# Attention probabilities split by query and turned by DMA, with slots of their own in a hand-written order

## The reference

```python
u = rmsnorm(h); proj = u @ w_in        # columns of attention A, attention C and the mixer B
oa = banded_attention(qa, ka, va, 128, 1, ...)          # 4 heads of 64, with sinks
for window, dil in ((128, 1), (512, 4), (2048, 16)):    # attention C, 4 heads, keys by stride
    o, s = dilated_banded_attention(qc, kc, vc, window, dil, tab_c)
# banded attention, per block of 128 queries, keys of this block and of the previous one:
logits = einsum('nbqhgd,nbshd->nbhgqs', qb, kb) + bias
probs = exp(logits - max); out = einsum('nbhgqs,nbshd->nbqhgd', probs, vb) / sum(probs)
xbc, z -> causal_dwconv, silu, ssd_chunked (chunks of 128 tokens), gated rmsnorm      # mixer B
h = h + concat(oa, ob, oc) @ w_out
h = h + square(relu(rmsnorm(h) @ w_up)) @ w_down
```

## Time and profile before

| | |
|---|---|
| median of 3 runs | 2439.88 us (2436.4 to 2441.14) |
| profiled run | 2438.68 us, span 2436.8 us |
| TensorE busy | 2354.4 us, 97% |
| VectorE / ScalarE / GpSimd busy | 1194.3 / 838.8 / 296.0 us |
| DMA | 419.64 MB, queue q1 56.9% of 16 engines |
| column stage | about 308 to 677 us |
| MLP stage | from about 740 us on |

### The profile page before, as it was taken

How to read it: one execution, slowest core, us unless ns; L and a number is a source line. 1 busy time by engine, 2 the same in 40 slices (tenths; PEclk the granted TensorE clock), 3 DMA queues, 4 the chain that set the end, 5 groups by cost and what they waited for, 6 DMA issues and landing times. The chain is left out here.

```text
span 2436.8 us, 42346 instructions
## 1 busy us (share of the span) xinstructions
PE 2354.4 (97%) x17150; PEld 1363.1 (56%) x17150; DVE 1194.3 (49%) x2673; ACT 838.8 (34%) x1579; POOL 296.0 (12%) x317
## 2 busy tenths in 40 slices
PE   9899889999899999999999999999999999999999
PEld 5456445554345555444555554445555456888887
DVE  5567465655647666742655563145555522322222
ACT  5544244555445454331433321033334111210210
POOL 0111223112011212001121100101111001000000
PEclk9999999999999999999999999999999999999999
DMA  7646496785477867884565564445554553222222
GB/s 254 238 168 226 169 231 174 211 233 178 144 228 201 218 208 230 257 266 159 141 159 160 166 200 153 158 132 128 159 173 156 177 162 117 88 96 96 96 96 85
DMA packets 396561, 419.64 MB, mean 172 GB/s; under 512 B 130319, under 2 KB 325391, under 8 KB 396112
## 3 DMA queue, kind: packets, MB, share of 16 engines
q1 hardware_dynamic: 396368, 416.94, 56.9%
HBM read 280.01 MB, written 118.96 MB: 164 GB/s over the span
## 5 line engine op out<-in xcount | busy, mean ns | idle before, releaser
L2423 PE MATMUL core_dense<-core_u,tok_ring 128*128 128x512 f16 (+2 forms) x4800 | 863.9, 340 | 7.8 <-DVE core_u L2008 7.5
L2423 PEld LDWEIGHTS core_dense<-core_u,tok_ring 128*128 128x128 f16 x4800 | 465.8, 98 | 377.9 <-DVE core_u L2008 11.4
L2423 PE MATMUL core_dense<-core_r_hi,tok_ring 128*128 128x512 f16 (+2 forms) x2560 | 650.1, 339 | 1.7 <-DVE core_r_lo L2027 1.7
L2423 PE MATMUL core_dense<-core_r_lo,tok_ring 128*128 128x512 f16 (+2 forms) x1280 | 434.1, 339 | 0.0
L2423 PEld LDWEIGHTS core_dense<-core_r_hi,tok_ring 128*128 128x128 f16 x2560 | 250.4, 98 | 196.8 <-DVE core_r_lo L2027 2.7
L2423 PE MATMUL core_dense<-tok_u,tok_ring 128*128 128x512 f16 x1104 | 257.7, 390 | 14.8 <-PEq L811 10.9
L1806 ACT ACTIVATE core_r<-core_dense 128x512 f32<-128x512 f32 (+2 forms) x160 | 82.2, 514 | 472.2 <-PE core_dense L2423 472.1
L2024 DVE TENSOR_TENSOR core_r<-core_r 128x512 f32<-128x512 f32 (+2 forms) x160 | 96.7, 604 | 291.1 <-ACT core_r L1806 290.7
L732 PE MATMUL tok_prod<-tok_w_hi,tok_u 128*128 128x512 f16 (+1 forms) x768 | 196.3, 345 | 4.1 <-DVE tok_u L601 4.1
L2423 PEld LDWEIGHTS core_dense<-tok_u,tok_ring 128*128 128x128 f16 x1104 | 107.3, 100 | 146.0 <-issue 24.8
L2423 PEld LDWEIGHTS core_dense<-core_r_lo,tok_ring 128*128 128x128 f16 x1280 | 125.2, 98 | 93.9 <-issue 0.7
(11 more groups left out here) (318 smaller groups left out, 2593.8 us busy)
## 6 DMA issues: line engine op xcount, KB each, us to landing
tok_ring<-scratch_kept_w SPq DMA_DIRECT2D x262, 512.0 KB, 4.5
scratch_kept_w<-tok_ring SPq DMA_DIRECT2D x72, 512.0 KB, 5.6
core_staged<-in_w_up SPq DMA_DIRECT2D x32, 512.0 KB, 4.7
core_staged<-in_w_down SPq DMA_DIRECT2D x32, 512.0 KB, 4.3
out_tok<-tok_tok SPq DMA_DIRECT2D x16, 644.0 KB, 3.0
core_piece<-in_c_kt SPq DMA_DIRECT2D x32, 288.0 KB, 3.9
core_piece<-in_c_v SPq DMA_DIRECT2D x16, 576.0 KB, 4.4
scratch_sums<-core_o SPq DMA_DIRECT2D x64, 132.0 KB, 3.7
```

The costliest lines, as they stand in the source:

```text
L2423: ins = pe.matmul(bank, w[:, k, part, :], s, start=first and j == 0, stop=last and j == 2, skip_group_check=True)
```

## The change

Attention's unit is cut into three with slots of their own: `S` (scores, bias, maxima, exponential), `T` (halves and turn) and `O` (product with the values, store). In `T` ScalarE and VectorE split `p` as it stands, by query, into `p_half` in SBUF, and two transposing DMAs on SyncE's queue write its turned form `p_t`, again in SBUF. TensorE's transposes, banks 3 and 4 for them and `p_hi`, `p_lo` are gone; the product uses bank 4. The plan is new:

- first 16 tiles: one every four quarters, `T` two and `O` six quarters after `S`; the 12 of the first block: one every five; MLP stage: one every two units, `T` one and `O` three units after `S`.
- the scans no longer stand behind all attention but among it, a chunk every 14 quarters or 10 units; the sums for the joins have a slot of their own (`sums`).
- the bias has two slots and is loaded once per run of tiles of one kind (`bias_runs`); the sampled keys always use banks 3 and 0.

```diff
+        def place_attention(beside, group, at, step, halved, valued):
+            was = None
+            for n in reals[group]:
+                beside[at].append(("S", n, 0, 0))
+                if was is not None:
+                    beside[at - step + valued].append(("O", was, 0, 0))
+                beside[at + halved].append(("T", n, 0, 0))
+                was, at = n, at + step
+            beside[at - step + valued].append(("O", was, 0, 0))
+            return at
...
-            for slot in att_slots(0, att_end[0]):
-                beside[at].append(slot)
-                at += 3
-            for n, slot in enumerate(att_slots(att_end[0], att_end[1])):
-                beside[at].append(slot)
-                at += 4 - n % 2
+            at = place_attention(beside, 0, 4 * COL_AHEAD + 1, 4, 2, 6)
+            last = place_attention(beside, 1, at + 3, 5, 2, 6)
...
-                beside[at].insert(0, first)
-                beside[at + 7].append(second)
-                at += 11
-                beside[at].append(third)
+                beside[at + 6 + 14 * c].insert(0, first)
+                beside[at + 13 + 14 * c].append(second)
+                beside[at + 17 + 14 * c].append(third)
+            beside[last + 3].append(("sums", 0, 0, 0))
+            at = last + 7
...
+                    some = [[] for _ in range(56)]
+                    at = place_attention(some, b + 2, HOST_FROM[b], 2, 1, 3)
+                    some[at + 3].append(("sums", 4 * b + 4, 0, 0))
+                    for c in range(4):
+                        for part, unit in zip((3, 6, 8), scan_parts(4 * b + 4 + c)):
+                            some[10 * c + part].append(unit)
...
+                def turn_p(n):
+                    e, many = real_no[n], 8 if att[n][4] else 4
+                    if e:
+                        sp.wait_ge(o_done, e)
+                    for i, ready in enumerate((hi_ready, lo_ready)):
+                        sp.wait_ge(ready, e + 1)
+                        sp.dma_start_transpose(p_t[:, i, 0:many, :], p_half[:, i, 0:many, :].rearrange("p a c -> p (a c)")).then_inc(pt_in[i], 16)
...
+                def high(n):
+                    e = real_no[n]
+                    act.wait_ge(p_ready, e + 1)
+                    if e:
+                        act.wait_ge(pt_in[0], 16 * e)
+                    src, dst = p_of(n, 0)
+                    act.activation(dst, src, ACT.Copy).then_inc(hi_ready, 1)
...
+                def low(n):
+                    e = real_no[n]
+                    dve.wait_ge(hi_ready, e + 1)
+                    if e:
+                        dve.wait_ge(pt_in[1], 16 * e)
+                    src, dst = p_of(n, 1)
+                    dve.tensor_tensor(dst, src, p_of(n, 0)[1], ALU.subtract).then_inc(lo_ready, 1)
...
-                    pe.wait_ge(lo_ready, 2 * e + 2)
+                    for i in range(2):
+                        pe.wait_ge(pt_in[i], 16 * (e + 1))
```

259 lines of the change are left out of this document (110 added, 149 removed).

## The result

The changed kernel takes 2530.93 us (median of 4 runs, 2525.18 to 2534.66), the kernel before 2439.80: a ratio of 1.037, with a 95% interval of 1.0352 to 1.0383. That lies above the stated range (2417 to 2505). The direction was forecast, the size was not: 10 us were forecast, 91 measured. The profiled execution took 2525.2 us, with a span of 2522.6.

A forecast was written before the change was run, and what follows sets the result against it. TensorE, busy 2354.4 of 2436.8 us, was taken as the bound. Terms: -56 + 32 + 19 + 21 + 7 - 6.5 - 3 = +13, set to +10 for overlap: 2449 us forecast, range 2417 to 2505.

The forecast's parts named there:

- Removed, 56 us: TensorE's transposes of the probabilities leave: 17 us in the column stage, about 39 in the MLP stage.
- The turn: Two transposing DMAs per tile on SyncE's queue: issue 1.0 and landing 3.5 us for half-size tiles, 1.2 and 5 otherwise.
- rival A: Faster: turns land like a small store, the second DMA within 2.5 us in the column stage; say 2422 us, chance 0.27.
- First 16 tiles, 32 us: Column stage: TensorE's value product waits for the turn, 12 us at eight tiles and 20 at four with SiLU ahead.
- 12 tiles, 19 us: First block's tiles in the column stage: product waits 7, SiLU 6, first chunk's load 3, shared PSUM banks 3 us.
- MLP stage, 21 us: 36 tiles: no wait for the turn; scan behind scores 14, sampled tokens' transposes 2, delayed low half 5 us.
- rival C: SyncE's queue becomes the bound, each turn holding it 6.1 us: 2690 us, chance 0.08; sign: issues of 3 us and more.
- Clock, 7 us: TensorE's lower clock after the four or five long waits of the column stage, 1.7 us per stretch.

The follow-up runs named there:

- e17: Changed kernel with the column stage's attention, and the scans, sums and joins that hang on it, three quarters later: 2503.7 us, ratio 1.0262 to the kernel before.
- e7: Changed kernel without the turning DMAs, the product reading a tile of ones (computes other values), new places kept: 2485.4 us.
- e6: Changed kernel with 116 idle matmuls ahead of the value product of 14 tiles of the column stage: 2525.5 us.
- e14: e9 with halves and product 2 and 4 units behind the scores and the sampled splits ahead of the scores: 2410.8 us, ratio 0.9877 to the kernel before.
- e15: Changed kernel at the places of the kernel before, without the turning DMAs, the product reading ones (computes other values): 2466.9 us.
- e5: Changed kernel with the scan's first part in PSUM banks 3 and 5 in place of 1 and 2: 2529.6 us.
- e8: Changed kernel with turns ahead of the store of the tile before on SyncE's queue, and SiLU behind the attention's steps: 2524.3 us.
- e4: Columns at the earlier kernel's places, TensorE turning, but VectorE's low half ahead of the next scores; MLP stage as in the changed kernel: 2481.1 us.
- e9: Columns as in the kernel before, scores ahead of the low half; MLP stage turned by DMA at the change's distances, scans behind the attention: 2447.0 us.

## Why the prediction was wrong

**Removed, 56 us:** right (59.2 by the group), and hidden in TensorE's busy time by the slower clock.

**The turn:** issue 1.0 to 1.2 us was about right in the columns (1.27); the landing was taken too long there (3.5 against a median of 2.5 in the first 16 tiles) and about right in the MLP stage (5 against 5.2 in its first block and 5.1 in the next, with issues of 2.2 and 1.5). So the condition of rival A was met, a landing within 2.5 us in the columns, and the kernel is still 91 us slower: that condition decided nothing.

**First 16 tiles, 32 us:** 28.1 by the DMA and 2.6 by the values' low half, near enough, with the most at the first tile (7.4). But the term was a list of waits of TensorE. By e17, 23 us of the columns hang on the quarter in which the attention stands (turned by DMA; no run shifts it where TensorE turns). I had put the convolution into the chain of eight tiles, and did not ask what another quarter would give, or that the kernel before, with a step of three, meets a different place of the column with each tile.

**12 tiles, 19 us:** 54.3 by waits: 36.7 at the product (33.3 for the turn, 3.4 for the values) against 13, the chunk's load 7.3 against 3, scores and scan in one bank 10.3 against 3. The chain was counted with 1 us for the convolutions in it. ScalarE's waits for VectorE's maxima from 308 to 740 us point to more, in the kernel before and in the changed one (total, times, longest):

```profile
ACT core_p L1836 <- DVE core_neg L2075: 58.2, 22, 5.2
```

```profile
ACT core_p L1843 <- DVE core_neg L2091: 102.7, 26, 11.8
```

ScalarE stands in order behind each of these waits, with the drains that VectorE's convolutions need.

**MLP stage, 21 us:** idle time rose by 34 us (27.7 to 61.7). The six waits of the scan behind the scores are there, 11.5 us for 14. The turn waits 10.4 us where none was forecast (issues of 2.2 us in the median and 3.8 at most, the sign of rival C in a mild form), yet taking the turn away (e7) shortens the stage by 4 only. The sampled halves, 18.6 against 4.6 before, were missing.

**Clock, 7 us:** the largest miss by account. Idle time rose by 93.6 us (82.4 to 176.0), transposes took away 59.2, the span grew by 85.8: so some 51 us went to the lower clock. By the windows above, less the transposes, about 28 of them are in the columns and most of the rest in the MLP stage. But e6 took 19 of those 28 away and the columns were as long as before: there most of it is no cost of its own, TensorE was slow while others were late. In the MLP stage e14, with the same matmuls and a clock of 1.00, needs 14 us less of TensorE than the changed kernel.

**The step that failed** is therefore the frame of the sum: waits of TensorE priced one by one, and the moves counted at nothing unless a wait was found for them. The removed work was taken as a gain that stays. In place of that the runs show a chain that is late by itself: with no turn at all the time is still 104 us (e7) and 86 us (e15) above the 2381 that were to be had, and the product waits for VectorE's low half. What is late is the row of hand-overs between ScalarE and VectorE, more than the load of either: in the columns VectorE is busy for 229 of 436 us, ScalarE for 186. Once it sets the pace, TensorE's saved time turns into idle time, and a wait that is mended (e5, e8) comes back at another step. The prediction's opening, TensorE busy 97% so that everything there counts one for one, is right for the kernel before and not for what the change makes of its columns.

**What stays open:** of the columns' 83 us over 353, the turn has 36 (e7) and the phase 23 (e17), and the two may overlap. With TensorE turning, the order of low half and scores costs 21 (e4 against e9), and at the old places the same order may be about half of e15's 45. At the new places the rest isn't attributed. What e7 and e15 have in common against the kernel before is the halves made in SBUF, whole tiles at a time, the probabilities held in their one buffer until the low half is made, the new banks and the bias loads; no run separates these. A second buffer for the probabilities, which would let VectorE score ahead of the low half with the DMA too, wasn't tried.

## What to carry to other kernels

Moving work off the busiest engine pays where the others have slack at that very place: in e14, with the turn by DMA in the MLP stage alone and room around each step, 27 of 39 us show, while in the columns no placement tried here gained. Before a step is moved, lay its period over the period of the work it stands among, and look on each in-order engine at what it now always stands behind. And price a change by a run without the new step at all: here that would have shown first that more is lost in the steps around the turn (104 us) than to the turn itself (some 45).

## What the hardware showed

- A transposing DMA from SBUF to SBUF of 128x512 in fp16 landed 2.4 us after its issue at least and 2.5 in the median (first 16 tiles, DMA engines busy for a share of 0.78), near the 2.1 us of a plain store of 128 KB, and its issue took 1.19 us at least. One of 128x1024 had an issue of 1.23 us at least. In the first block of the MLP stage (DMA share 0.98) its issue had a median of 2.2 us and its landing of 5.2, in the next (0.85) 1.5 and 5.1. The Trainium skill (VectorE: DVE Perf Modes, section "The three transpose paths") gives 1309 ns for a 128x128 block of bf16 by DMA. Here four such blocks of fp16 landed in 2.5 us, issue included, half of what four times that figure would be.
- Filling TensorE's waits with idle matmuls lifted its granted clock from 0.87 to 0.94 in a stage of 435 us and changed the stage by 0.5 us.
